# Dilated attention with queries and keys ordered by parity in two of its three groups

## Chip, core and metric

The kernel runs on one core of a Trainium2 chip. The metric is the device time of one execution in microseconds (us); a kernel's time is the median of its runs. The core has a matrix engine (PE, TensorE; its weight loads are listed apart as PEld), a vector engine (DVE), a scalar engine (ACT), GpSimd (POOL) and a queue engine (SP) that issues most transfers. Each engine executes its own instructions in order and waits on semaphores for the others.

## What is computed

Two blocks of transformer layers on 256 tokens of width 1024. The change touches one stage, the attention of the second layer of the first block, with 16 heads of 64 dimensions and three groups of keys. In short:

```python
DIL_CONFIGS = ((128, 1), (512, 4), (2048, 16))       # (window, dilation)

def dilated_group(q, k, v, window, dilation):
    """query t attends t, t-d, t-2d, ..., t-window"""
    ...
    logits = jnp.where(valid[None, None], logits, -jnp.inf)
    lse = jax.nn.logsumexp(logits, axis=-1)
    p = jnp.exp(logits - lse[..., None])
    return jnp.einsum("bhqk,bqkhd->bqhd", p, vb), lse

def dilated_attention(h, cos, sin, w_in, q_gain, k_gain, w_out):
    proj = (h @ w_in).reshape(B, S, N_DIL_GROUPS, 3, H, hd)
    for g, (window, dilation) in enumerate(DIL_CONFIGS):
        q = apply_rope(rms_norm(proj[:, :, g, 0], q_gain[g]), cos, sin)
        k = apply_rope(rms_norm(proj[:, :, g, 1], k_gain[g]), cos, sin)
        o, lse = dilated_group(q, k, proj[:, :, g, 2], window, dilation)
        ...
    alpha = jax.nn.softmax(jnp.stack(lses, axis=0), axis=0)
    o = jnp.sum(alpha[..., None] * jnp.stack(outs, axis=0), axis=0)
    return o.reshape(B, S, H * hd) @ w_out
```

Weighting the groups by their denominators is the same as one softmax over the scores of all three groups side by side, and that is what the kernel does. With dilations 4 and 16 a query meets only keys whose position differs from its own by an even number.

## The kernel before

A planner (`Plan`, `Program`) writes one list of steps. Five functions (`sp_program`, `pe_program`, `act_program`, `dve_program`, `pool_program`) then walk over that list, and each emits its engine's part. So the order on every engine is the order of the list; the waits are tokens (semaphore, value) that the planner gives out, among them `self.free[bank]`, the token after which one of the eight PSUM banks may be written again. A bank holds 512 fp32 values per partition. Banks G0 to G3 and D0 to D3 are used.

Weights stream through six slots (`raw`); ACT and DVE split each into a high and a low half (`whi`, `wlo`, line 1674 for DVE), and three matmuls (high x high, low x high, high x low) stand for one fp32 product. This is nearly all of the program.

The dilated stage goes over 8 heads at a time (`hh` 0 and 1). For each half:

- `dil_in` runs nine times (group g, part r: queries, keys, values). `token` multiplies tokens by a weight unit: 48 matmuls with a 128x128 piece of `xhi` or `xlo` (tokens t*128 to t*128+127) as the stationary operand and 512 weight columns moving. Queries and keys then pass through `head_norm`, are transposed on PE (`head_turn`, line 1453) into D0 and D1, and ACT copies them to `dqT` or `dkT` (64 dimensions of two heads x 256 tokens, four such pairs). Values are copied by ACT to `dv` (`keep_v`).
- `dil_attn` runs `attention` over eight steps p: pair of heads c = p // 2, query tile qt = p % 2. Tile qt has 128 queries and kl = 128 * (qt + 1) keys per group, so n = 384 or 768 scores per query. In `step_of(p)` the list gets: `scores(p)` and the two `bias` steps (DVE adds the mask `dmask` and takes the row's minimum, line 1774), `values(p - 2)`, then for each head w `turn` of the step before (PE transposes the weights `S`, line 1418, and ACT copies them to `PT`) and `exp` of this step (ACT), and the two `weigh` steps (DVE: reciprocal, line 1779, and product, line 1782). `values` multiplies `dv` by `PT` into G2 or G3; after the second query tile of a pair ACT copies the output (`doT`, or `xhi` in half 1, with `xlo` by DVE at line 1786).

For n = 768 a head's scores take two banks: `score_bank` returns D0 for the first head of every step and D2 for the second, and `turn` uses G0 and G1 together. All matmuls stand in the profile under line 1265, all ACT operations under line 1487, since helpers emit them; the tiles' names tell them apart. Matmuls on plain fp32 are recorded twice, transposes once.

Of the kernel before, what the change touches and what calls it, by code (L numbers as in the profile page):

```python
# [6 lines left out]
F32 = mybir.dt.float32  # L7
# [34 lines left out]
class Plan:  # L42
# [150 lines left out]
    def token(self, need):  # L193
        b0, b1 = self.next_pair()
        bank_free = [self.free[b0], self.free[b1]]
        for k0 in (0, 4):
            pc = self.take()
            tok = self.ev("pe", "piece")
            self.add("token", b0=b0, b1=b1, k0=k0, c=pc["c"], w_lo=pc["w_lo"], need=[need(k0 + kk) for kk in range(4)],
# [184 lines left out]
    def attention(self, name, klen, ready, emit, bias_ready=None, row=False, ng=1, compact=False, after=None):  # L384
# [3 lines left out]
        def score_bank(p, w):  # L388
            if compact:
                return D0 + w  # L390
            return D0 + 2 * w if ng > 1 else D0 + 2 * (p % 2) + w

        def scores(p):
            kl = klen(p % 2)
            n = kl * ng
            nb = -(-n // 512)
            banks = [score_bank(p, w) for w in range(2)]
            bank_free = [self.free[banks[w] + b] for w in range(2) for b in range(nb)]
            tok = self.ev("pe", "score")
            self.add("scores", name=name, p=p, kl=kl, n=n, nb=nb, banks=banks, bank_free=bank_free, row=row,  # L400
                     ready=ready[:-1] if first[0] else [])
            first[0] = False
            for w in range(2):
                j = 2 * p + w
                td = self.ev("dve", "biased")
                self.add("bias", name=name, j=j, n=n, nb=nb, bank=banks[w], score=tok, s_free=self.s_free[j % 4],
                         ready=bias_ready(2 * (p // 2) + w) if bias_ready else None)
                for k in range(nb):
                    self.free[banks[w] + k] = td
# [12 lines left out]
        def turn(j):  # L422
            n = rec[j][1]
            bt = G0 if n > 512 else G0 + j % 2
            banks = (G0, G1) if n > 512 else (bt,)
            tok, te = self.ev("pe", "turned"), self.ev("act", "pt")
            self.add("turn", name=name, j=j, n=n, bt=bt, nb=len(banks), weighed=rec[j][0], bank_free=[self.free[b] for b in banks],
                     turned=tok, pt_free=self.pt_free[j % 2])
            self.s_free[j % 4] = tok
            for b in banks:  # L430
                self.free[b] = te
# [47 lines left out]
    def emit_split(self, dst, c0, res):  # L479
        def emit(c, bank, tok):  # L480
            hi, lo = self.ev("act", "o_hi"), self.ev("dve", "o_lo")
            self.add("o_split", dst=dst, c=c0 + c, bank=bank, value=tok, o_hi=hi)
# [11 lines left out]
    def mix_attention(self, hh, name, compact, **kw):  # L494
# [8 lines left out]
        self.attention(name, lambda qt: P * (qt + 1), self.at, self.emit_split("x", 4, res), **kw)  # L503
# [85 lines left out]
class Program(Plan):  # L589
# [62 lines left out]
    def dil_attn(self, hh):  # L652
        self.mix_attention(hh, ("dil", hh), compact=False, ng=3)
# [79 lines left out]
    def na_attn(self, i):  # L733
        self.ya_split = [None] * 4
        steps = self.attention(("na", 0), lambda qt: T, self.nat, self.emit_split("ya", 0, self.ya_split),
# [371 lines left out]
def build(nc, a, out):  # L1107
    root = ExitStack()
    with root:
# [72 lines left out]
        with ExitStack() as c:  # L1182
# [8 lines left out]
            dil_mask = named("dmask", [P, 1152], F32, c)  # L1191
            dil_gn = named("dgn", [P, 2, 3, 64], F32, c)
            attn["dil"] = scratch(c, 768)
# [47 lines left out]

        def angle(n):
            return rp[:, n, :, :]
# [858 lines left out]
```

## Time and profile before

| | us |
|---|---|
| median of 3 runs | 2361.69 |
| lowest, highest | 2361.56, 2369.41 |
| the profiled execution's own time | 2364.49 |
| its span (first to last instruction) | 2363.2 |
| attention of half 0, in the span | about 965.7 to 1010.7 |
| attention of half 1, in the span | about 1120.1 to 1165.5 |

The page of the profile gives each engine's busy time and share of the span, the chain of work that ended last, and the costliest groups of instructions. PE is busy for 2260.6 us (96%), DVE for 1327.0, ACT for 1155.3. The ends of matmuls are modelled, so a busy PE is not PE at its peak; the starts are measured, and the distance from one start to the next is the better measure of pace. PEclk is the share of the full TensorE clock that was granted.

### The profile page before, as it was taken

To read this page: it belongs to the slowest core of one execution; us is meant where nothing else is said; L and a number is where in the kernel's file an instruction comes from. 1 tells how busy PE (TensorE), PEld (TensorE's weight loads), DVE (VectorE), ACT (ScalarE), POOL (GpSimd) and SP (SyncE) were. 2 spreads that over 40 slices of the span, in tenths; PEclk is the share of its full clock that TensorE was granted. 3 is DMA by queue.
4 is the path that set the end of the run, shared out by engine and by line. 5 is a ranking of instruction groups with operands and counts; after the bars stand their busy time and mean duration, and the time that the engine had idled before them with its cause. 6 is when DMAs were issued, how large, how long until landed. Compare 5 with 4: busy or idle time off the path is not lost.

```text
span 2363.2 us, 38278 instructions
## 1 busy us (share of the span) xinstructions
PE 2260.6 (96%) x16752; PEld 2060.3 (87%) x16752; DVE 1327.0 (56%) x1763; ACT 1155.3 (49%) x1348; POOL 57.2 (2%) x72
## 2 busy tenths in 40 slices
PE   6999998999999999899899999999999999999998
PEld 3999866999999987677699997899999988989998
DVE  2543565544455466657555445556786555667873
ACT  3443565543444354544554335654555456436553
POOL 2000000000000000000000011000000020000000
PEclk9999999999999999999999999999999999999999
DMA  8767562666575756345165555433655363445550
GB/s 311 236 229 289 196 250 68 218 223 231 187 252 196 266 192 247 128 150 205 56 214 183 192 196 175 161 125 125 211 182 191 126 233 132 154 143 179 179 196 19
DMA packets 273590, 439.75 MB, mean 186 GB/s; under 512 B 10656, under 2 KB 147152, under 8 KB 273296
## 3 DMA queue, kind: packets, MB, share of 16 engines
q1 hardware_dynamic: 270880, 429.07, 52.6%
q0 software_dynamic: 2256, 7.12, 0.9%
q8 instruction: 132, 2.16, 0.4%
q10 hardware_dynamic: 288, 1.11, 0.1%
q14 instruction: 34, 0.28, 0.0%
HBM read 436.22 MB, written 1.05 MB: 185 GB/s over the span
## 4 chain that ended last, share of the span: by engine, by line
PE 89%; ACT 5%; DVE 3%; DMA 1%; issue 1%; SPq 0%; POOL 0%; ACTq 0%; POOLq 0%; DVEq 0%
PE ps L1265 86%; ACT whi L1487 1%; DVE wlo L1674 1%; PE ps L1418 1%; ACT PT L1487 1%; PE ps L1365 1%; PE ps L1453 1%; DMA raw<-in_mod_w 1%; ACT xhi L1487 1%; PE ps L1428 1%; ACT L1487 1%; ACT S L1487 0%; DMA raw<-in_fox_w_in 0%; SPq L1254 0%; ACT x L1487 0%
## 5 line engine op out<-in xcount | busy, mean ns | idle before, releaser
L1674 DVE TENSOR_TENSOR wlo<-raw,whi 128x2048 fp32r<-128x2048 f32 x339 | 769.0, 2275 | 584.8 <-ACT whi L1487 584.6
L1487 ACT ACTIVATE whi<-raw 128x2048 fp32r<-128x2048 f32 x339 | 640.7, 1895 | 422.4 <-PE ps L1265 387.1
L1265 PE MATMUL ps<-xhi,whi 128*128 128x256 f32 x2888 | 733.5, 286 | 14.8 <-ACT xhi L1487 11.4
L1265 PE MATMUL ps<-xhi,wlo 128*128 128x256 f32 x2888 | 727.9, 284 | 0.0
L1265 PEld LDWEIGHTS ps<-xhi,whi 128*128 128x128 f32 x2888 | 555.7, 192 | 29.1 <-issue 27.6
L1265 PEld LDWEIGHTS ps<-xhi,wlo 128*128 128x128 f32 x2888 | 555.8, 192 | 0.3
L1265 PE MATMUL ps<-xlo,whi 128*128 128x256 f32 x2888 | 471.0, 284 | 3.6 <-DVE xlo L1892 3.4
L1265 PEld LDWEIGHTS ps<-xlo,whi 128*128 128x128 f32 x2888 | 401.4, 192 | 4.3 <-DVE xlo L1892 3.8
L1265 PE MATMUL ps<-hhi,whi 128*128 128x256 f32 x1056 | 299.0, 283 | 0.9 <-DVE modc L1687 0.9
L1265 PE MATMUL ps<-hlo,whi 128*128 128x256 f32 x1056 | 298.5, 283 | 0.0
L1265 PE MATMUL ps<-hhi,wlo 128*128 128x256 f32 x1056 | 297.5, 282 | 0.0
L1265 PE MATMUL ps<-whi,xhi 128*128 128x512 f32 x608 | 242.1, 398 | 7.0 <-DVE wlo L1674 4.5
L1265 PE MATMUL ps<-wlo,xhi 128*128 128x512 f32 x608 | 237.7, 391 | 0.0
L1265 PEld LDWEIGHTS ps<-hhi,whi 128*128 128x128 f32 x1056 | 199.6, 189 | 5.0 <-issue 3.4
L1265 PEld LDWEIGHTS ps<-hhi,wlo 128*128 128x128 f32 x1056 | 199.1, 189 | 0.1
L1265 PEld LDWEIGHTS ps<-hlo,whi 128*128 128x128 f32 x1056 | 197.9, 187 | 0.0
L1265 PE MATMUL ps<-whi,xlo 128*128 128x512 f32 x608 | 187.9, 390 | 0.0
L1265 PEld LDWEIGHTS ps<-whi,xhi 128*128 128x128 f32 x608 | 114.8, 189 | 37.1 <-issue 8.5
L1265 PEld LDWEIGHTS ps<-whi,xlo 128*128 128x128 f32 x608 | 114.3, 188 | 24.5
L1265 PEld LDWEIGHTS ps<-wlo,xhi 128*128 128x128 f32 x608 | 114.8, 189 | 22.4
L1487 ACT ACTIVATE e<-ps 128x512 f32<-128x512 f32 (+1 forms) x48 | 30.4, 634 | 158.3 <-PE ps L1265 158.2
L1487 ACT ACTIVATE hhi<-e 128x512 fp32r<-128x512 f32 x66 | 41.7, 632 | 110.0 <-DVE e L1936 71.2
(222 smaller groups left out, 1999.6 us busy)
## 6 DMA issues: line engine op xcount, KB each, us to landing
raw<-in_mod_w SPq DMA_DIRECT2D x72, 1024.0 KB, 9.2
raw<-in_w_in SPq DMA_DIRECT2D x52, 1024.0 KB, 4.9
raw<-in_ffn_w_gate SPq DMA_DIRECT2D x88, 512.0 KB, 6.5
raw<-in_ffn_w_up SPq DMA_DIRECT2D x88, 512.0 KB, 7.8
raw<-in_ffn_w_down SPq DMA_DIRECT2D x44, 1024.0 KB, 6.7
raw<-in_w_up SPq DMA_DIRECT2D x88, 512.0 KB, 4.7
raw<-in_dil_w_in SPq DMA_DIRECT2D x36, 1024.0 KB, 5.9
raw<-in_w_down SPq DMA_DIRECT2D x22, 1024.0 KB, 4.8
```

Of the source, the lines that this page charges most:

```text
L1265: return nc.tensor.matmul(o, lhs, rhs, start=start, stop=stop, skip_group_check=True)
L1365: ins = nc.tensor.transpose(ps[:, s["bank"], m * P:(m + 1) * P], mrow[:, m * P:(m + 1) * P], ident[:, :])
L1418: ins = nc.tensor.transpose(o, w["S"][:, s["j"] % 4, b * P:(b + 1) * P], ident[:, :])
L1428: ins = nc.tensor.transpose(ps[:, D2, h * T + b * P:h * T + (b + 1) * P], w["S"][:, j, b * P:(b + 1) * P], ident[:, :])
L1453: ins = nc.tensor.transpose(ps[:, D0 + c // 2, (c % 2) * T + t * P:(c % 2) * T + (t + 1) * P], tms[s["name"]][:, t, c * P:(c + 1) * P], id ...
L1487: return nc.scalar.activation(o, i, func, **kw)
L1674: V.tensor_tensor(wlo[:, s["c"], 0:s["n"]], raw[:, s["slot"], 0:s["n"]], whi[:, s["c"], 0:s["n"]].bitcast(F32), ALU.subtract).then_inc(sem ...
```

## The change

In groups 1 and 2 (dilations 4 and 16) queries and keys are put in order by parity, even positions first. The scores of these groups are computed for pairs of equal parity alone. For query tile qt this takes, per head and group, two matmuls (parity r = 0, 1) of 64 queries by kl / 2 keys in place of one of 128 by kl. The scores of a head are now n = 2 * kl = 256 or 512, so they fit into one bank.

- `score_bank` returns D0 + 2 * (p % 2) + w, so steps of even and odd p use different banks; `turn` uses one bank, G0 + j % 2, for every tile.
- The scores after the first kl are laid out in blocks of 128: 64 keys of group 1, then 64 keys of group 2. Transposed, a block has group 1's weights on partitions 0 to 63 and group 2's on 64 to 127. To match, `keep_v` of groups 1 and 2 fills `dv` of 1 and 2 crosswise, in two copies of 64 partitions each; a values matmul sums over both groups at once, for 64 queries of one parity.
- `token` for the values of groups 1 and 2 takes its tokens by parity: the stationary operand is every second column of `xhi` or `xlo`.
- `head_turn` writes all queries (group 0 too) in the order of parity within each tile of 128, and the keys of groups 1 and 2 in the order of parity over all 256; ACT reads the transposed values in PSUM with a step of two.
- The outputs come out in the order of parity within each tile of 128. ACT and DVE put them back when they write `doT`, `xhi` and `xlo` (`scattered`, `gathered`).
- The mask has 768 columns in place of 1152, in the new order.

```diff
@@ planner
-    def token(self, need):
+    def token(self, need, by_parity=False):
...
         def score_bank(p, w):
             if compact:
                 return D0 + w
-            return D0 + 2 * w if ng > 1 else D0 + 2 * (p % 2) + w
+            return D0 + 2 * (p % 2) + w
 
         def scores(p):
             kl = klen(p % 2)
-            n = kl * ng
-            nb = -(-n // 512)
+            n = 2 * kl if dilated else kl
             banks = [score_bank(p, w) for w in range(2)]
-            bank_free = [self.free[banks[w] + b] for w in range(2) for b in range(nb)]
+            bank_free = [self.free[b] for b in banks]
...
         def turn(j):
             n = rec[j][1]
-            bt = G0 if n > 512 else G0 + j % 2
-            banks = (G0, G1) if n > 512 else (bt,)
+            bt = G0 + j % 2
...
-        b0, b1, tok = self.token(self.need_x)
+        b0, b1, tok = self.token(self.need_x, by_parity=r == 2 and g > 0)
@@ PE, token
+            def tokens(t, kc, half, by_parity):
+                return (t[:, kc, :].rearrange("p (i r) -> p r i", r=2)[:, half, :] if by_parity else
+                        t[:, kc, half * P:(half + 1) * P])
@@ PE, scores
                     for g, (qT, kT, _) in enumerate(groups(s["name"])):
-                        for w in range(2):
-                            bk, off = s["banks"][w] + (g * kl) // 512, (g * kl) % 512
-                            ins = mm(ps[:, bk, off:off + kl], qT[64 * w:64 * w + 64, c, qt * P:(qt + 1) * P],
-                                     kT[64 * w:64 * w + 64, c, 0:kl], True, not s["row"])
+                        if g == 0:
+                            for w in range(2):
+                                h = slice(64 * w, 64 * w + 64)
+                                ins = mm(ps[:, s["banks"][w], 0:kl], qT[h, c, qt * P:(qt + 1) * P], kT[h, c, 0:kl], True,
+                                         not s["row"])
+                            continue
+                        for r in range(2):
+                            for w in range(2):
+                                h = slice(64 * w, 64 * w + 64)
+                                o = ps[64 * r:64 * r + 64, s["banks"][w], kl:2 * kl].rearrange("p (f g i) -> p g f i", g=2, i=64)
+                                ins = mm(o[:, g - 1, :, :], qT[h, c, qt * P + 64 * r:qt * P + 64 * r + 64],
+                                         kT[h, c, P * r:P * r + kl // 2].rearrange("p (f i) -> p f i", i=64), True, True)
@@ PE, values
+                    for f in range(nb if dilated else 0):
+                        b = nb + f
+                        for r in range(2):
+                            for w in range(2):
+                                hd, o = 2 * c + w, 64 * r
+                                ins = mm(ps[64 * w:64 * w + 64, s["bank"], qt * P + o:qt * P + o + 64],
+                                         every[1 + f][2][:, r, hd * 64:(hd + 1) * 64], PT[:, w, b * P + o:b * P + o + 64],
+                                         False, f == nb - 1)
@@ ACT, head_turn
+                    if s["dst"][0] == "dil" and s["dst"][1] == "q":
+                        act(dst[:, :, :].rearrange("p c (t r i) -> p (c t) r i", t=2, r=2),
+                            turned.rearrange("p b (c t i r) -> p (b c t) r i", c=2, t=2, r=2), ACT.Copy).then_inc(sem["head_kept"])
@@ ACT, keep_v
+                    if s["name"] in (("dil", 1), ("dil", 2)):
+                        h = 64 * s["name"][1] - 64
+                        act(qkv["dil", "v", 1][h:h + 64, :, :], ps[0:64, s["b0"]:s["b0"] + 2, :], ACT.Copy)
+                        act(qkv["dil", "v", 2][h:h + 64, :, :], ps[64:P, s["b0"]:s["b0"] + 2, :],
+                            ACT.Copy).then_inc(sem["v_kept"])
```

PE's instructions in steps 3 and 4 of half 0, before (S are the scores and then the weights of one head, PT their transpose, ps is PSUM; 128x256 is the output's shape, x5 a count, and "waits" names the semaphores: biased by DVE, pt by ACT, weighed by DVE):

```order
L1265 MATMUL ps<-dkT,dqT 128x256 [waits biased]
L1265 MATMUL ps<-dkT,dqT 128x256 x5
L1265 MATMUL ps<-PT,dv 64x128 [waits pt]
L1265 MATMUL ps<-PT,dv 64x128 x11
...
L1418 MATMUL ps<-ident,S 128x128 [waits weighed]
L1418 MATMUL ps<-ident,S 128x128 x5
L1418 MATMUL ps<-ident,S 128x128 [waits pt,weighed]
L1418 MATMUL ps<-ident,S 128x128 x5
```

The same place now:

```order
L1268 MATMUL ps<-dkT,dqT 128x256 [waits biased]
L1268 MATMUL ps<-dkT,dqT 128x256
L1268 MATMUL ps<-dkT,dqT 64x2x64 x8
L1268 MATMUL ps<-PT,dv 64x128 [waits pt]
L1268 MATMUL ps<-PT,dv 64x128 x3
L1268 MATMUL ps<-PT,dv 64x64 x8
...
L1432 MATMUL ps<-ident,S 128x128 [waits weighed]
L1432 MATMUL ps<-ident,S 128x128 x3
L1432 MATMUL ps<-ident,S 128x128 [waits weighed]
L1432 MATMUL ps<-ident,S 128x128 x3
```

Scores go from 6 to 10 matmuls, values stay at 12, the transposes of a head go from 6 to 4, and the second head's transposes no longer wait for ACT's copy (pt). Over the whole program PE has the same order otherwise.

PE at the head of half 0's attention, before (mod_row is ACT's copy out of bank D2 or D3, head_kept its copy of the transposed keys):

```order
L1265 MATMUL ps<-dkT,dqT 128x128 [waits mod_row,head_kept]
L1265 MATMUL ps<-dkT,dqT 128x128 x5
L1265 MATMUL ps<-dkT,dqT 128x256 [waits mod_col,biased]
L1265 MATMUL ps<-dkT,dqT 128x256 x5
L1418 MATMUL ps<-ident,S 128x128 [waits hn_mul,weighed]
```

and now:

```order
L1268 MATMUL ps<-dkT,dqT 128x128 [waits head_kept]
L1268 MATMUL ps<-dkT,dqT 128x128
L1268 MATMUL ps<-dkT,dqT 64x64 x8
L1268 MATMUL ps<-dkT,dqT 128x256 [waits mod_col,mod_row]
L1268 MATMUL ps<-dkT,dqT 128x256
L1268 MATMUL ps<-dkT,dqT 64x2x64 x8
L1432 MATMUL ps<-ident,S 128x128 [waits hn_mul,weighed]
```

The scores of step 1 have moved ahead of the bias of step 0: they no longer wait for it.

ACT ahead of the same attention, before:

```order
L1487 ACTIVATE dkT<-ps 128x1024
L1487 ACTIVATE dv<-ps 128x1024
L1487 ACTIVATE whi<-raw 128x2048
L1487 ACTIVATE mrow<-ps 128x512
L1487 ACT_TABLE_LOAD
```

and now:

```order
L1509 ACTIVATE dkT<-ps 128x1024
L1509 ACTIVATE dv<-ps 64x1024 x2
L1509 ACTIVATE whi<-raw 128x2048
L1509 ACTIVATE mrow<-ps 128x512
L1509 ACT_TABLE_LOAD
```

The copy of the values has become two, ahead of the weight split (`whi`) and of everything that attention asks of ACT.

## Rows read from the trace of the kernel before

**Rows 1.** Stretches: length; PE, PEld, DVE, ACT, POOL busy us; PEclk, DMA share, GB/s.
```profile
850.00:965.00 115.00, 113.76 (x561) 89.90 (x563) 80.73 (x111) 59.03 (x59) 1.65 (x3) 1.00 0.62 226
...
965.67:976.80 11.13, 5.55 (x43) 4.20 (x42) 7.00 (x15) 7.35 (x13) 0.00 (x0) 0.85 1.00 365
...
985.72:994.64 8.92, 7.23 (x79) 5.73 (x79) 5.45 (x17) 5.89 (x14) 0.00 (x0) 1.00 0.01 2
...
1003.56:1010.73 7.17, 5.28 (x49) 4.33 (x49) 1.11 (x3) 2.39 (x4) 0.00 (x0) 0.81 0.01 2
...
1120.14:1131.52 11.38, 6.92 (x43) 5.28 (x42) 6.71 (x20) 8.45 (x17) 0.00 (x0) 0.67 0.53 176
```

**Rows 2.** Chain of waits, part of a cycle of half 0: start us, us, what.
```profile
983.28 0.49 PE ps L1418 x3
...
983.79 0.49 ACT PT L1487
984.28 0.91 ACT S L1487 x2
985.20 0.39 ACT PT L1487
```

**Rows 3.** Timeline of PE, half 0: start us, us, line, op, count [idle before].
```profile
963.75 1.92 PE L1265 MATMUL ps<-raw,csil 128*32 128x512 f32 x16
...
980.25 1.57 PE L1265 MATMUL ps<-dkT,dqT 64*128 64x256 f32 x12
...
981.75 1.53 PE L1265 MATMUL ps<-PT,dv 128*64 128x128 f32 x24
...
983.21 0.88 PE L1418 MATMUL ps<-ident,S 128*128 128x128 f32 x6
...
985.72 0.88 PE L1265 MATMUL ps<-PT,dv 128*64 128x128 f32 x12 [0.47 <-ACT PT L1487]
...
986.53 0.87 PE L1418 MATMUL ps<-ident,S 128*128 128x128 f32 x6
...
988.39 0.85 PE L1418 MATMUL ps<-ident,S 128*128 128x128 f32 x6 [0.99 <-ACT PT L1487]
```

**Rows 4.** ACT, whole span, by shape: busy us, mean ns of one, idle before.
```profile
L1487 ACT ACTIVATE S<-S,nm 128x256 f32<-128x256 f32 x48 | 23.9, 501 | 5.2 <-DVE nm L1774 5.1
...
L1487 ACT ACTIVATE S<-S,nm 128x768 f32<-128x768 f32 x16 | 14.9, 929 | 0.0
...
L1487 ACT ACTIVATE PT<-ps 128x512 f32<-128x512 f32 x20 | 12.0, 599 | 33.0 <-PE ps L1428 33.0
...
L1487 ACT ACTIVATE PT<-ps 128x256 f32<-128x256 f32 x12 | 4.5, 379 | 6.6 <-PE ps L1428 4.4 <-PE ps L1418 2.2
```

**Rows 5.** DVE, whole span, by shape.
```profile
L1782 DVE TENSOR_SCALAR S<-S,ri 128x256 f32<-128x256 f32 x48 | 18.8, 391 | 1.7
...
L1774 DVE CUSTOM_DVE_ANT_0 S<-ps,dmask 128x768 f32<-128x768 f32 x16 | 14.6, 952 | 2.9 <-PE ps L1265 2.9
L1774 DVE CUSTOM_DVE_ANT_0 S<-ps,nbias 128x256 f32<-128x256 f32 x32 | 12.3, 421 | 4.7 <-PE ps L1265 4.7
...
L1782 DVE TENSOR_SCALAR S<-S,ri 128x768 f32<-128x768 f32 x16 | 9.9, 621 | 0.6
```

**Rows 6.** Timeline at the head of half 0's attention.
```profile
964.78 1.02 ACT L1487 ACTIVATE dv<-ps 128x1024 f32<-128x1024 f32 x1
...
968.23 0.94 PE L1265 MATMUL ps<-dkT,dqT 64*128 64x128 f32 x12 [2.55 <-ACT mrow L1487]
969.84 0.55 DVE L1774 CUSTOM_DVE_ANT_0 S<-ps,dmask 128x384 f32<-128x384 f32 x1
```

**Rows 7.** Timeline of a projection: starts of a load and of two matmuls.
```profile
1012.54 0.19 PEld L1265 LDWEIGHTS ps<-wlo,xhi 128*128 128x128 f32 x1
1012.76 0.40 PE L1265 MATMUL ps<-wlo,xhi 128*128 128x512 f32 x1
...
1013.00 0.39 PE L1265 MATMUL ps<-whi,xhi 128*128 128x512 f32 x1
```

More of the change, by code:

```diff
@@ L198, in token @@
             tok = self.ev("pe", "piece")
-            self.add("token", b0=b0, b1=b1, k0=k0, c=pc["c"], w_lo=pc["w_lo"], need=[need(k0 + kk) for kk in range(4)],
+            self.add("token", by_parity=by_parity, b0=b0, b1=b1, k0=k0, c=pc["c"], w_lo=pc["w_lo"], need=[need(k0 + kk) for kk in range(4)],
                      bank_free=bank_free if k0 == 0 else [])
@@ L382, in attn_begin, with attention @@
         self.pt_free = [None] * 2
-    def attention(self, name, klen, ready, emit, bias_ready=None, row=False, ng=1, compact=False, after=None):
+    def attention(self, name, klen, ready, emit, bias_ready=None, row=False, dilated=False, compact=False, after=None):
         rec = []
@@ L405, in scores @@
                 td = self.ev("dve", "biased")
-                self.add("bias", name=name, j=j, n=n, nb=nb, bank=banks[w], score=tok, s_free=self.s_free[j % 4],
+                self.add("bias", name=name, j=j, n=n, bank=banks[w], score=tok, s_free=self.s_free[j % 4],
                          ready=bias_ready(2 * (p // 2) + w) if bias_ready else None)
-                for k in range(nb):
-                    self.free[banks[w] + k] = td
+                self.free[banks[w]] = td
                 rec.append([td, n, kl])
@@ L477, in attention, with emit_split @@
         return []
-    def emit_split(self, dst, c0, res):
+    def emit_split(self, name, dst, c0, res):
         def emit(c, bank, tok):
             hi, lo = self.ev("act", "o_hi"), self.ev("dve", "o_lo")
-            self.add("o_split", dst=dst, c=c0 + c, bank=bank, value=tok, o_hi=hi)
+            self.add("o_split", name=name, dst=dst, c=c0 + c, bank=bank, value=tok, o_hi=hi)
             self.free[bank] = lo
@@ L734, in na_attn @@
         self.ya_split = [None] * 4
-        steps = self.attention(("na", 0), lambda qt: T, self.nat, self.emit_split("ya", 0, self.ya_split),
+        steps = self.attention(("na", 0), lambda qt: T, self.nat, self.emit_split("na", "ya", 0, self.ya_split),
                                bias_ready=lambda h: self.bias_ready[h // 2], compact=True)
@@ L1240, in flat, with scattered, gathered @@
             return t[:, k0:k1, :].rearrange("p k n -> p (k n)")
+        def scattered(o, name):
+            return o.rearrange("p (t i r) -> p t r i", t=2, r=2) if name == "dil" else o
+        def gathered(o, name):
+            return o.rearrange("p (t r i) -> p t r i", t=2, r=2) if name == "dil" else o
         def angle(n):
@@ L1438, in pe_program @@
                     PT = attn[s["name"][0]]["PT"]
-                    tot = nb * len(every)
-                    for b in range(tot):
+                    dilated = len(every) > 1
+                    for b in range(nb):
                         for w in range(2):
@@ L1443, in pe_program @@
                             ins = mm(ps[64 * w:64 * w + 64, s["bank"], qt * P:(qt + 1) * P],
-                                     every[b // nb][2][:, b % nb, hd * 64:(hd + 1) * 64], PT[:, w, b * P:(b + 1) * P],
-                                     b == 0, b == tot - 1)
+                                     every[0][2][:, b, hd * 64:(hd + 1) * 64], PT[:, w, b * P:(b + 1) * P],
+                                     b == 0, b == nb - 1 and not dilated)
+                    for f in range(nb if dilated else 0):
[6 more added lines that the diff above has]
+                                         False, f == nb - 1)
                     ins.then_inc(sem["value"])
@@ L2025, in constants @@
     parts = []
+    parity, nth = q // 64, q % 64
     for qt in range(2):
-        for window, dil in ((128, 1), (512, 4), (2048, 16)):
-            d = (q[:, None] + P * qt) - np.arange(P * (qt + 1))[None, :]
+        kl = P * (qt + 1)
+        query = (P * qt + 2 * nth + parity)[:, None]
+        same = 2 * np.arange(64)[None, :] + parity[:, None]
+        keys = [(np.broadcast_to(np.arange(kl), (P, kl)), 128, 1)]
+        for half in range(qt + 1):
+            keys += [(same + P * half, 512, 4), (same + P * half, 2048, 16)]
+        for key, window, dil in keys:
+            d = query - key
             parts.append(np.where((d >= 0) & (d <= window) & (d % dil == 0), 0.0, BIG).astype(np.float32))
```

55 lines of the change are left out of this document (31 added, 24 removed).

## The prediction, made before the changed kernel ran

> **What bounds the kernel now.** I read the page first, then the busy time by stretch. Nearly everywhere PE sets the time: in the projections ahead of the first dilated attention it is busy for 113.76 of 115 us, while ACT works for 59.03 and DVE for 80.73 [rows 1]. The two dilated attentions are the exception. Half 0's runs from 965.67 to 1010.73, 45.1 us; half 1's has the same instructions. In a steady stretch of two steps (a cycle: one pair of heads, both query tiles) PE works for 7.23 of 8.92 us, ACT for 5.89, DVE for 5.45 [rows 1]: no engine is full, so a loop of waits sets the pace.
>
> The chain of waits shows the loop: transposes on PE, the copy of the weights to PT on ACT (0.49 us), an exponential (0.91), the second copy (0.39), values on PE [rows 2]. After the tile of 768 scores it is worse: the second head's transposes wait 0.99 us for the first head's copy, since both use banks G0 and G1 (at 988.39) [rows 3]. Transfers are out of it: in the steady cycle the DMA engines are busy for 0.01 [rows 1], because the six slots are full. What attention gives back should therefore come off the end.
>
> **Pace of PE.** 12 value matmuls take from 981.75 to 983.21, 1.46 us, and 6 take from 985.72 to 986.53, 0.81 [rows 3]. So one costs (1.46 - 0.81) / 6 = 0.108 us, and a block costs another 0.16 for the change to the next kind of matmul. One of 128 columns on half the array in 0.108 us, two halves side by side, means 0.216 if it were alone. Six score matmuls of 256 columns take 1.50 us (980.25 to 981.75): 0.216 each and 0.20 for the change. The modulation matmuls, which use a quarter of the array's columns, are 8 of 512 columns in 1.92 us (at 963.75) [rows 3]; alone they would be 8 x 4 x 0.216 = 6.9, so four do run side by side.
>
> **The change part by part, per cycle.**
>
> Transposes: 18 become 12, at 0.108 each: 0.65 us less on PE. Some of it is in the loop (below).
>
> Values: of 18 matmuls of 128 columns 6 stay, 12 now have 64 columns. At half the price each this saves 0.22 us for the first tile and 0.43 for the second, and makes the blocks 0.59 and 1.03 us. If a floor per instruction held, nothing is saved.
>
> Scores: 2 matmuls stay per step, 4 become 8 of a quarter of the area, which use a quarter of the array (64 rows, 64 columns). No row shows that shape. Bounds for the second tile: with four side by side 2 x 0.216 + 8 x 0.054 + 0.20 = 1.06; with two, 1.49; one at a time, 2.36. One more change of shape adds 0.16 to each. For the first tile half the work: 0.79 to 1.44, where before it was 0.85. I take four side by side, as in the modulation row: 1.22 and 0.79. The scores have a window to hide in, while ACT works.
>
> The Trainium skill speaks against this part: "TensorEngine Tiling (Array Packing)", Key Properties, says that changing the tiling mode drains the engine, and a step now has one such change more. Its 64×64 mode has four tiles that run at once. The trace agrees as far as it goes: the block's fixed 0.16 and 0.20 us above are such changes, and they are small against the wait removed.
>
> Elementwise work shrinks by a third. From the slopes between 256 and 768 columns [rows 4, 5]: an exponential of 512 takes 0.715 us, bias 0.69, product 0.47; a copy of 512 is 0.60; those of 256 are 0.50, 0.42, 0.39 and 0.38. ACT's cycle falls to about 5.1 us, DVE's to about 4.4.
>
> Banks: scores of the next step no longer wait for the bias of this one, nor the second head's transposes for the first's copy. What is late next? The PE-ACT loop: values of the first tile 0.59; transposes 0.87 (at 986.53) [rows 3] less two of 0.108, and 0.04 to the copy's start, 0.69; copy 0.51 until the next can start; exponential 0.50; copy 0.60; hand-over 0.13 (ACT's copy of 985.20 ends at 985.59, PE starts at 985.72 [rows 2, 3]); values 1.03; transposes beside the copy of the output 0.45; copy 0.28; exponential 0.70; copy 0.38; hand-over 0.13. Sum 5.99. The DVE-ACT loop (product, next bias, exponential, copy, exponential, for both tiles) is 0.47 + 0.39 + 0.69 + 0.42 + 2 x (0.50 + 0.715) + 0.60 + 0.38 = 5.4, with reciprocals and hand-overs, which I estimate at 0.9, 6.3. PE alone: scores 2.0, values 1.6, transposes 1.6, so 5.2. I take 6.3 for the cycle; 5.9 is the least, and with one-at-a-time scores about 7.5 the most.
>
> Three whole cycles per half: 2 x 3 x (8.92 - 6.3) = 15.7 us.
>
> Head of the attention: scores of step 0 no longer wait 2.55 us for ACT's mrow copy out of a bank they don't use now [rows 6], and those of step 1 not for the bias. But keep_v is two copies of as many columns; I take each as long as the one (1.02 [rows 6]; the least would be half of it). They stand ahead of the weight split, whose DVE part stands ahead of the bias. So the bias starts at 970.9, not 969.84 [rows 6]. Then bias to 971.3, two exponentials and products until 973.1, bias of step 1 ready at 973.9, exponential, copy and hand-over: values of step 0 at 975.1, against 976.80 [rows 1]: 1.7 us gained. In half 1 (11.38 us now) the same, and more of it at half clock: 2.0. The two other double copies are covered by PE's full projections.
>
> Tail: after the last cycle 7.17 us in half 0 [rows 1]. Now 0.59 + 0.69 + 0.51 + 0.60 + 0.13 + 1.03 = 3.55, and about 1 more where PE is at half clock (0.81 there [rows 1]): 2.6 less. For half 1 I take about the same, 5.0 in all.
>
> Reordering copies: ten copies of transposed queries and keys read PSUM with a step of two. Nothing in the trace shows such a read; bounds are the present 1.02 us and twice that. Eight lie under projections with ACT half idle; the last of each half is in the path: 0 to 2.0 in all, I take the middle, 1.0. Outputs written with a step of two: 0.38 us each, same bounds, hidden beside transposes.
>
> Strided stationary operand: 4 units x 48 = 192 matmuls of 512 columns. They start 0.23 us apart (1012.76, 1013.00) and a load takes 0.19, under the matmul before [rows 7]. Lower bound nothing; at twice the duration (0.38) 0.15 x 192 = 29 us; I take nothing, the value of the only rows with such loads. The mask's smaller transfer is nothing: DMA has room.
>
> In the Trainium skill, "Advanced Engine Details and Errata", SBUF Cachelines, lines are 16 bytes and two hits per line suffice; a step of two fp32 gives just two, so by it these loads cost nothing. By its section PSUM Cachelines a line there is 8 bytes, so a step of two fp32 uses one element of each, and the last reordering copies would stand in the sum with 2.0 instead of 1.0. No row of this case shows either.
>
> **Sum.** 15.7 + 3.7 + 5.0 - 1.0 = 23.4 us. The profiled execution took 2364.5 (span 2363.2 and 1.3 around it), so 2341; it was 2.8 above the median of 2361.7, and against that median the forecast is 2338.5.
>
> **Rivals.**
>
> A. Quarter-array matmuls gain nothing from each other, or PE's instructions (88 per cycle in place of 78) come no faster. For it: the shape is new here. Against: modulation. Cycle 7.5 us: 2 x 3 x 1.4 = 8.5, with head and tail 16 us, 2346.
>
> B. Slower: strided weight loads. If a step of two makes a load three times as long, 0.57 us, PE starts every 0.57 instead of 0.23 in 192 matmuls: 65 us lost, 2404. It eats the gain from 0.23 + 23.4 / 192 = 0.35 us per load; a result slower than before by 0.5% needs 0.41. For it: no row with a step. Against: so large a factor.
>
> C. PE falls to half clock inside the cycles, because it has less to do. For it: at the head, with PE busy 6.92 of 11.38 us, the clock was 0.67 [rows 1]. Against: 7.23 of 8.92 kept 1.00, and 5.2 of 6.3 is the same share. At half clock PE alone needs some 9.5 us: 2 x 3 x 0.6 = 3.5 lost, head and tail gained (8.7 - 1.0): 2357.
>
> D. The gain is hidden anyway, for the next stage waits for something else. Against: 0.01 DMA share, full slots. about 2360.
>
> **Chances.** Forecast 0.79, its own range 2332 to 2345; A 0.10; B 0.05; C 0.04; D 0.02. 0.5% is 11.8 us, about what a measurement tells from no change. Faster by more 0.88, within 0.06 (C, D and the edge of B), slower 0.06. Range for 8 in 10: 2331 to 2350, which takes in A.
>
> **What would show it.** Cycles from one block of first-tile values to the next near 6.3 us, at clock 1.00; no wait of transposes for PT; scores of step 1 before the bias of step 0; score blocks of the second tile near 1.2 us; the 64-row copies at 1.0; matmuls of by-parity tokens still 0.23 apart. Wrong, if these last are further apart, if copies of dqT exceed 2 us, or if cycles stay above 8 us.

## Result and profile after

The changed kernel takes 2339.2 us (median of 4 runs, 2337.9 to 2341.9), the kernel before 2361.9 beside it. The ratio is 0.9894, 95% interval 0.9882 to 0.9906: 25 us (22 to 28) less. The two medians themselves are 22.7 us apart. The forecast was 2338.5 us. The profiled execution took 2341.9 us, with a span of 2340.6, 22.6 less than before.

The table compares starts in the two traces (us).

| stretch | before | after | gained | predicted |
|---|---|---|---|---|
| ahead of the dilated stage (its first matmul at 854.62, 855.97) | | | -1.35 | 0 |
| four by-parity units, first to last start of a unit | 10.75 | 11.05 | -1.2 | 0 |
| head, half 0 (copy of dkT to first values) | 12.94 | 11.45 | 1.5 | 1.7 - 0.5 |
| head, half 1 | 11.34 | 9.47 | 1.9 | 2.0 - 0.5 |
| three cycles, half 0 | 26.76 | 19.25 | 7.5 | 7.9 |
| three cycles, half 1 | 28.05 | 19.57 | 8.5 | 7.9 |
| tails (last first-tile values to next projection) | 7.17, 5.88 | 3.82, 3.82 | 5.4 | 5.0 |
| first unit of half 1's projections, to the start of the next | 11.71 | 11.37 | 0.3 | - |
| sum | | | 22.6 | 23.4 |

The first row is not the change, since both kernels run the same instructions up to there. It is what is left of two differences: within the first 50 us of the span the changed kernel's execution gains 4.0 us (why is open), and between 300 and 412 us, around the attention ahead of this stage, it loses 5.4, with 0.92 of the clock granted where the kernel before had 0.98. Stretches of the kernel before, then of the changed one (length; PE, PEld, DVE, ACT, POOL busy; PEclk, DMA share, GB/s):

```profile
300.00:412.00 112.00, 103.39 (x624) 77.57 (x621) 63.97 (x165) 64.27 (x132) 0.00 (x0) 0.98 0.44 156
```

```profile
300.00:412.00 112.00, 105.74 (x601) 79.24 (x601) 60.45 (x162) 61.26 (x128) 0.00 (x0) 0.92 0.40 140
```

The changed kernel's heads, steady cycle, tail and half 1's first cycle:

```profile
965.88:977.33 11.45, 6.72 (x81) 3.43 (x81) 5.89 (x16) 9.69 (x15) 0.00 (x0) 0.79 0.83 304
984.22:990.40 6.18, 5.60 (x88) 4.17 (x89) 4.24 (x17) 4.48 (x14) 0.00 (x0) 1.00 0.01 3
996.58:1000.40 3.82, 2.96 (x45) 2.39 (x45) 0.95 (x3) 1.75 (x4) 0.00 (x0) 1.00 0.00 0
1110.15:1119.62 9.47, 4.58 (x64) 2.96 (x64) 5.02 (x19) 8.51 (x17) 0.00 (x0) 0.80 0.62 204
1119.62:1126.83 7.21, 6.71 (x92) 5.29 (x89) 4.42 (x18) 4.30 (x14) 0.00 (x0) 0.79 0.01 2
```

The steady cycle (984.22 to 990.40) takes 6.18 us, where [rows 1] have 8.92. PE's share rose from 7.23 of 8.92 to 5.60 of 6.18. The two heads ran at 0.79 and 0.80 of the clock, and in half 1 so did the first cycle (7.21); half 0's first cycle took 6.89 us at 0.86.

PE in the steady cycle of the changed kernel, start and duration, idle time before and its releaser in brackets:

```profile
984.22 0.67 PE L1268 MATMUL ps<-PT,dv 128*64 128x128 f32 x12 [0.51 <-ACT PT L1509]
984.82 1.39 PE L1432 MATMUL ps<-ident,S 128*128 128x128 f32 x8
986.14 1.30 PE L1268 MATMUL ps<-dkT,dqT 64*128 64x256 f32 x20
987.37 1.12 PE L1268 MATMUL ps<-PT,dv 128*64 128x128 f32 x24
988.42 0.66 PE L1432 MATMUL ps<-ident,S 128*128 128x128 f32 x4
989.01 0.88 PE L1268 MATMUL ps<-dkT,dqT 64*128 64x128 f32 x20
```

Start to start: values 0.60 and 1.05 us (0.59 and 1.03 predicted), scores of the second tile 1.23 (1.22). The second head's transposes no longer wait 0.99 us for PT [rows 3]; what is left is 0.51 us for PT ahead of the first tile's values. The chain of waits through the same cycle (start, duration, what; "S x2" is an exponential with the reading of its sum):

```profile
984.81 0.18 DVE ri L1818
...
985.01 0.50 DVE S L1821
...
985.55 0.66 PE ps L1432 x4
986.21 2.31 PE ps L1268 x44
...
988.54 0.42 ACT doT L1509
988.95 0.33 ACT PT L1509
989.28 0.70 ACT S L1509 x2
989.98 0.27 ACT PT L1509
990.26 0.71 ACT S L1509 x2
```

It is one loop through all three engines: the second head's exponential, its reciprocal and product on DVE, its transposes, the scores and values of the second tile on PE, then on ACT the copy of the output (doT), a copy to PT, the first head's exponential and the other copy to PT. The predicted loops, PE-ACT (5.99) and DVE-ACT (6.3), each hold a part of it, and neither holds the second tile's scores.

### The profile page after: what moved, and what is told of

It is laid out like the page before. It is cut to its first block, busy times and chain, and to the rows that moved or that the text cites. A ratio compares the mean times of both kernels' runs of the same rounds, so it can differ in the third digit from the quotient of the medians.

```text
span 2340.6 us, 38441 instructions
## 1 busy us (share of the span) xinstructions
PE 2247.2 (96%) x16832; PEld 2049.3 (88%) x16832; DVE 1317.4 (56%) x1763; ACT 1148.6 (49%) x1352; POOL 61.2 (3%) x72
## 3 DMA queue, kind: packets, MB, share of 16 engines
q0 software_dynamic: 2192, 6.92, 0.8%
HBM read 436.02 MB, written 1.05 MB: 187 GB/s over the span
## 4 chain that ended last, share of the span: by engine, by line
PE 89%; ACT 5%; DVE 3%; DMA 1%; issue 1%; SPq 0%; POOL 0%; ACTq 0%; POOLq 0%; DVEq 0%
PE ps L1268 86%; ACT whi L1509 1%; DVE wlo L1713 1%; ACT xhi L1509 1%; PE ps L1475 1%; PE ps L1372 1%; DMA raw<-in_mod_w 1%; ACT S L1509 1%; ACT L1509 1%; PE ps L1442 1%; PE ps L1432 1%; DMA raw<-in_fox_w_in 0%; ACT PT L1509 0%; SPq L1257 0%; ACT x L1509 0%
```

## Experiments

Each ratio is to the kernel before, run beside the experiment. Totals of one kernel differ by some us between executions, with the clock granted in stages that no kernel here touches. So each experiment is read first from one stretch of its trace, from the dilated stage's first matmul to the last values of half 1. That is 309.37 us before and 285.99 in the changed kernel: 23.4 less.

**One pair of banks for the transposes (e1), for the scores (e2), for both (e9).**

```diff
@@ e1, transposes of 512 columns also wait for the other head's copy
                     q.wait_ge(s["bank_free"])
+                    q.wait_ge(s["other"])
@@ e2
-            return D0 + 2 * (p % 2) + w
+            return D0 + 2 * w if dilated else D0 + 2 * (p % 2) + w
```

> Takes away the second buffer of the transposes alone: a head's transposes of 512 columns also wait for the copy of the other head's weights, as they did before. Smaller tiles and the second pair of score banks stay. Theory S (the smaller tiles give most of the gain): after the first head's transposes (0.66 us with the product) the second's start some 0.5 to 0.6 us later, and this wait is paid once per cycle, since it stands in the loop: cycles 6.7 us in place of 6.18, in all 8 x 0.55 = 4.4 us given back of some 23, so ratio to the kernel before 0.991. Theory B (the free banks give most of it): the cycle goes back towards 8 us and more than 10 us are given back, ratio 0.994 or more. Theory H (the wait is hidden by exponentials): cycle 6.2, ratio 0.989.

> Takes away the second pair of score banks alone: scores of every step go to D0 and D2, so those of step p+1 wait for the bias of step p. Tiles and transposes stay as changed. Theory S: scores of the second tile start at most 0.1 us later (bias of the first tile is done when PE comes to them), those of the first tile about 0.4 us later, beside exponentials that they don't delay: cycle 6.2 to 6.4 us; at the head of each attention about 0.5 to 1.5 us more. In all 1 to 4 us given back, ratio 0.990 to 0.991. Theory B: cycle 7 us or more, ratio 0.993 or more.

> Both banks' doublings are taken away together (e1 and e2 in one kernel); only the smaller tiles and the matmuls of equal parity stay. If the two add up, the stretch from the first projection of the dilated stage to the last values of half 1 is 286.0 + 9.8 + 4.7 = 300.5 us (309.4 before): the smaller tiles alone give 8.9 of the 23.4 us and the banks 14.5; ratio about 0.996. If they overlap (the second head's transposes and the next scores wait in the same time), 297 us and ratio 0.994: smaller tiles 12, banks 11.

The stretch in e1, e2 and e9:

```profile
853.42:1149.25 295.83, 274.08 (x1744) 215.98 (x1744) 189.13 (x332) 156.44 (x212) 0.00 (x0) 0.96 0.50 179
```

```profile
852.51:1143.17 290.66, 272.21 (x1744) 215.05 (x1745) 189.07 (x332) 155.57 (x212) 0.00 (x0) 0.96 0.51 182
```

```profile
855.25:1150.45 295.20, 271.71 (x1745) 214.01 (x1745) 189.19 (x332) 156.24 (x212) 0.00 (x0) 0.96 0.51 179
```

e1 gives back 9.8 us (ratio 0.9929, 0.9913 to 0.9946). Theory S was right on the steady cycle, 6.85 us (PE below), and wrong on the sum. It allowed 0.55 us for each of 8 cycles; the first cycle of each half took 10.2 and 9.9 us, at 0.59 and 0.61 of the clock.

```profile
984.96 0.67 PE L1269 MATMUL ps<-PT,dv 128*64 128x128 f32 x12 [0.51 <-ACT PT L1511]
985.56 0.66 PE L1434 MATMUL ps<-ident,S 128*128 128x128 f32 x4
987.00 0.63 PE L1434 MATMUL ps<-ident,S 128*128 128x128 f32 x4 [0.78 <-ACT PT L1511]
987.56 1.30 PE L1269 MATMUL ps<-dkT,dqT 64*128 64x256 f32 x20
...
991.81 0.67 PE L1269 MATMUL ps<-PT,dv 128*64 128x128 f32 x12 [0.51 <-ACT PT L1511]
```

The third line shows the wait that came back. e2 gives back 4.7 us (ratio 0.9921, 0.9906 to 0.9937), mostly at the heads (13.36 and 11.00 in place of 11.45 and 9.47); its steady cycles are 6.29 to 6.37. Both together (e9) give back 9.2, not the sum of 14.5, and less than the 11 of the second guess; the ratio is 0.9941 (0.9927 to 0.9955).

Most of the 5.3 us between 14.5 and 9.2 is granted clock and not an overlap of waits. The first cycle of half 1, in e1 and then in e9:

```profile
1122.30:1132.20 9.90, 8.61 (x93) 6.35 (x89) 4.59 (x18) 4.42 (x14) 0.00 (x0) 0.61 0.01 2
```

```profile
1126.39:1133.24 6.85, 5.63 (x94) 4.18 (x89) 4.39 (x18) 4.40 (x14) 0.00 (x0) 1.00 0.00 0
```

With the second pair of score banks gone as well, the cycle is 3 us shorter, at full clock. The two first cycles together are longer than the changed kernel's by 6.0 us in e1, 0.6 in e2 and 2.3 in e9: 4.3 of the 5.3. Why e1's ran so long at half clock, no run shows. The waits themselves overlap by little: e1 adds 0.67 us to a steady cycle, e2 0.11 to 0.19, both together again 0.67 (988.07 to 994.92 in e9), so there the scores' wait falls into time that the transposes' wait has already made, but over four steady cycles that is 0.7 us.

So of 23.4 us in the stretch the free banks give 9.2 and the smaller tiles 14.2, as these traces stand. No run parts the 14.2 further, into PE's smaller matmuls and the shorter work of DVE and ACT. As e1 and e9 stand 0.6 apart, with other stretches of half clock, I would not read these closer than 1 or 2 us.

**Shape and number of score matmuls (e3, e4).**

```diff
@@ e3, one matmul of 128 queries in place of two of 64
-                        for r in range(2):
-                            for w in range(2):
...
+                        for w in range(2):
+                            h = slice(64 * w, 64 * w + 64)
+                            o = ps[:, s["banks"][w], kl:2 * kl].rearrange("p (f g i) -> p g f i", g=2, i=64)
+                            ins = mm(o[:, g - 1, :, :], qT[h, c, qt * P:(qt + 1) * P],
+                                     kT[h, c, 0:kl // 2].rearrange("p (f i) -> p f i", i=64), True, True)
@@ e4
-                                h = slice(64 * w, 64 * w + 64)
+                                h = slice(0, 64)
```

> Scores of groups 1 and 2 as 4 matmuls per step on 64 rows x 128 columns in place of 8 on 64 x 64; all 128 queries of a tile meet the keys of even position alone, so the queries of odd position have the wrong keys. The streamed work is the same if four quarter tiles do run side by side (8 x N / 4 = 4 x N / 2), and there is no change of shape within the block. Theory M (a change of shape costs 0.16 us): score block of the second tile 1.06 us in place of 1.23, of the first 0.65 to 0.70 in place of 0.79; cycle 6.0, since the second tile's block is in the loop; total 1 to 1.5 us less than the changed kernel. Theory N (the change of shape costs nothing, quarter tiles are a bit slower than four side by side): same direction but a block that starts its last matmuls at a uniform distance. Theory I (the number of instructions sets the block): 0.9 us or less.

> The quarter-array scores of both heads read their operands from partitions 0 to 63, so that only two of the four quarters of the array are used (both heads get the first head's scores in groups 1 and 2). Same instructions and sizes. Theory Q (four quarters run side by side when they may): now two do, each 128-column quarter matmul of the second tile takes 0.108 of PE's time in place of 0.054, block 1.23 + 8 x 0.054 = 1.66 us; first tile 0.79 + 0.22 = 1.0; cycle 6.18 + 0.43 = 6.6; total 3 to 4 us more than the changed kernel, ratio about 0.991. Rival P (what pairs up are columns alone, rows do not matter): blocks and cycle unchanged.

PE in a steady cycle of e3, then of e4:

```profile
982.47 1.15 PE L1268 MATMUL ps<-dkT,dqT 64*128 64x256 f32 x12
983.56 1.12 PE L1268 MATMUL ps<-PT,dv 128*64 128x128 f32 x24
```

```profile
987.40 1.77 PE L1268 MATMUL ps<-dkT,dqT 64*128 64x256 f32 x20
989.10 1.12 PE L1268 MATMUL ps<-PT,dv 128*64 128x128 f32 x24
```

e4's block is 1.70 us in place of 1.23 and its cycle 6.65 in place of 6.18 (stretch 290.79; ratio 0.9912, 0.9896 to 0.9928). The 0.47 more is what 8 matmuls cost when they run two abreast and not four: theory Q holds, and it is paid in full, since this block stands in the loop. e3's block is 1.09 and its cycle 6.04, 0.14 less. That is the price of one more change of shape (theory M), since the time is lost where the shape changes. From the last matmul of group 0 to the first of groups 1 and 2 it is 0.31 us in the changed kernel and 0.21 in e3, to the next one 0.16 and 0.11. Behind that the starts are 0.11 us apart in both, and in the changed kernel four matmuls start together each time, within 0.02 us. By the number of instructions (12 records for 20) the block would have fallen further. The Trainium skill, "TensorEngine Tiling (Array Packing)", Key Properties, has both: tiles operate independently, and a change of mode drains the engine. The trace agrees with both, by the 1.23 us beside 1.70 and by the 0.14. e3's total (ratio 0.9896, 0.9879 to 0.9913) can't show 0.8 us in six cycles, and its stretch (285.84) doesn't either.

**Stationary operands with a step (e8, e5).**

```diff
@@ e8
-        b0, b1, tok = self.token(self.need_x, by_parity=r == 2 and g > 0)
+        b0, b1, tok = self.token(self.need_x, by_parity=False)
@@ e5: step 4 and 8 in half 0, 16 and 3 in half 1
+                    k0 = min(kc, NC - (by_parity + 1) // 2)
+                    a = t[:, k0:, :].rearrange("p k n -> p (k n)")[:, 0:P * by_parity]
+                    return a.rearrange("p (i r) -> p r i", r=by_parity)[:, half, :]
```

> Values of groups 1 and 2 from tokens in their given order (stationary operand without a step; the values of the wrong tokens). Theory F: units 10.75 in place of 11.05 us, 4 x 0.30 = 1.2 us less than the changed kernel, 2338.0. Rival: the 0.3 us per unit is not the step but the longer double copy behind it: units stay at 11.05.

> The stationary operand of the four values units of groups 1 and 2 is read with other steps in place of 2: half 0 group 1 step 4, group 2 step 8; half 1 group 1 step 16, group 2 step 3 (wrong tokens, same number of matmuls and loads). In the changed kernel a unit of 48 matmuls with step 2 takes 11.05 us from first to last start, without a step 10.75. Theory L (a load pays per 16-byte line of 4 fp32 that it touches once it uses fewer than two elements of each): steps 4, 8 and 16 are alike and slower, up to 0.38 per load in place of 0.19: as the load then outlasts the matmul it becomes the pace, 0.38 us each, unit 18 us; step 3 in between. Theory F (a step costs the same small amount whatever its length, about 6 ns per matmul): all four units 11.05. Theory G (cost grows with the distance): 4 < 8 < 16.

In e8 the four units take 10.75 us: the 0.30 us per unit are the step, 1.2 in all. The stretch fell only by 0.7, because half 1's first cycle was slower (7.7 for 7.2, at 0.74 of the clock). The ratio, 0.9912 (0.9898 to 0.9925), is no better than the changed kernel's; a gain this small can't be read from it. Weight loads with steps of 4, 8, 16 and 3 (e5, one unit each; count, busy us, mean ns):

```profile
L1268 PEld LDWEIGHTS ps<-whi,xlo 128*128 128x128 f32 x16 | 4.4, 316 | 0.0
...
L1268 PEld LDWEIGHTS ps<-whi,xlo 128*128 128x128 f32 x16 | 4.6, 330 | 0.0
...
L1268 PEld LDWEIGHTS ps<-whi,xlo 128*128 128x128 f32 x16 | 4.3, 300 | 0.0
...
L1268 PEld LDWEIGHTS ps<-whi,xlo 128*128 128x128 f32 x16 | 3.9, 253 | 0.0
```

and with step 1 and 2 in the changed kernel (units at 904.46 and 916.24):

```profile
L1268 PEld LDWEIGHTS ps<-whi,xlo 128*128 128x128 f32 x16 | 3.0, 188 | 0.6
...
L1268 PEld LDWEIGHTS ps<-whi,xlo 128*128 128x128 f32 x16 | 3.1, 194 | 0.6
```

The load's own time follows theory L in kind: nearly nothing up to two elements per 16 bytes, then 253, 316, 330, 300. But the unit takes 11.05, 11.21, 11.32, 11.73 and 11.25 us for steps 2, 3, 4, 8 and 16. Loads recorded as 316 ns go with matmuls that start 241 ns apart on average (11.32 / 47). So the pace is not the load's duration, as theory L had it, and F and G fail too: the price is neither fixed nor does it grow with distance. Each of these steps was measured in one unit only; e5's ratio is 0.9898 (0.9875 to 0.9921, two runs). The Trainium skill, "Advanced Engine Details and Errata", SBUF Cachelines, says that it takes two hits on a line to absorb the latency; the loads' durations agree (188 and 194 ns against 253 to 330), and step 2 cost 6 ns per matmul, not nothing.

**The second copy of the values (e6).**

```diff
-                    if s["name"] in (("dil", 1), ("dil", 2)):
+                    if False:
```

> Values of groups 1 and 2 are kept by one copy of 128 partitions in place of two of 64 (halves of the parities are not crossed, so the values stand in the wrong place). Each copy of 64 partitions takes 1.02 us, as long as the one. Theory: the second copy is in the path at the head of both attentions, ahead of the weight split and bias of half 0 and ahead of the output split and the table load of half 1: 1.0 us each, 2.0 in all, total 2337.2 against 2339.2. Rival: something else is late there (the transfer, the transposed keys), gain 0 to 0.5.

The heads take 10.16 and 8.03 us in place of 11.45 and 9.47: 1.3 and 1.4 less, and the stretch 2.8 less (283.18). The theory holds (it expected 2.0), and the price is a little above one copy: after a copy of 128 partitions the next starts 0.92 us later (968.53 behind 967.61 below), while the two copies of 64 take 2.07 from 966.93 to 969.00 and start 1.05 behind that of dkT (965.88). ACT at the head of half 0, of e6 and then of the changed kernel:

```profile
967.61 1.02 ACT L1509 ACTIVATE dkT<-ps 128x1024 f32<-128x1024 f32 x1 [4.50 <-PE ps L1475]
968.53 1.02 ACT L1509 ACTIVATE dv<-ps 128x1024 f32<-128x1024 f32 x1
969.44 1.91 ACT L1509 ACTIVATE whi<-raw 128x2048 fp32r<-128x2048 f32 x1
```

```profile
965.88 1.02 ACT L1509 ACTIVATE dkT<-ps 128x1024 f32<-128x1024 f32 x1 [4.50 <-PE ps L1475]
966.93 2.04 ACT L1509 ACTIVATE dv<-ps 64x1024 f32<-64x1024 f32 x2
969.00 1.91 ACT L1509 ACTIVATE whi<-raw 128x2048 fp32r<-128x2048 f32 x1
```

The ratio, 0.9896 (0.9880 to 0.9913), is no different from the changed kernel's.

**The order at the head (e7), mirrored banks (e10), and filled waits (e11, e12).**

```diff
@@ e7: begun adds the last values' copies; ensure() half 0's weight split, which take(2) keeps from being planned earlier
-            pc = self.take(ahead)
+            pc = self.take(2 if (i, u) == (1, 13) else ahead)
...
+            if begun and p == 0:
+                begun()
...
+            if hh == 0 and p == 8:
+                self.ensure()
+            if hh == 1 and p in (2, 4, 6, 8):
+                self.split_chunk(p // 2 - 1, ("dil", 1), self.o_ready[p // 2 - 1])
@@ e10, with e7
-            bt = G0 + j % 2
+            bt = (G2 if mirror else G0) + j % 2
-            bank = D3 if compact else G2 + c % 2
+            bank = D3 if compact else (G0 if mirror else G2) + c % 2
@@ e11, with e10: n = 4 and 6 in half 0; 4, 4 and 6 in half 1
+                    for _ in range(s["n"]):
+                        mm(ps[:, s["bank"], :], xhi[:, 7, 0:P], flat(xhi, 5, 7), True, True)
```

> The full computation. ACT's order at the head of the dilated attention: the last values' copies stand behind the exponentials of step 0; half 0's weight split behind step 8's copies; in half 1 the four splits of the kept output stand one each behind steps 2, 4, 6, 8 in place of ahead of step 0. Theory: the head is a queue on ACT and DVE that nothing in attention needs. Half 0: bias of step 0 some 4 us earlier, exponentials wait for the table load instead (about 2.7 us earlier), values of step 0 about 7.7 us behind the start of the keys' copy in place of 11.45: 3.7 us. Half 1: 2.6 us. Splits in the cycles fall into ACT's 1 us of idle time: 0 to 0.3 each lost. Total 2339.2 - 5.5 = 2333.7, ratio 0.987. Rival: the copies only move into the loop ahead of PT and the head gains less than 2 us; or the later transfer starves the next projection: 2339 or more.

> e7 and, in half 1, transposes in G2 and G3 and values in G0 and G1, since the last projected values of half 1 stand in G0 and G1 and there the first transposes waited 2.61 us for their copies. First transposes of half 1 at 3.8 us behind the start of the keys' copy in place of 5.80, the copies of PT right behind the values' copies: values of step 0 at 7.1 us in place of 7.75: 0.6 us less. Rival: half clock comes a little later and takes it back: 0.

> e10 and matmuls of 128x512 on xhi that nobody reads, put into PE's waits at the head of each attention: 4 behind the scores of step 1, 6 behind those of step 2, in half 1 also 4 ahead of the scores of step 0, 0.23 us each. Theory C (the granted clock falls to half because PE waits so much at the head, and this costs more than the wait): the granted clock stays 1.00 through both attentions; cycle from the first values to the next 6.2 to 6.9 us in place of 8.3 and 7.4 in e7, so 2 to 3 us less than e10; ratio 0.986 or less. Rival D (the clock falls all the same, and the fillers stand in the way at half pace): 1 to 3 us more than e10.

> The changed kernel as it is, with matmuls of 128x512 on xhi that nobody reads in PE's waits at the head: half 0 12 ahead of the scores of step 1 and 6 behind them, half 1 4 ahead of the scores of step 0 and 15 behind those of step 1, each set shorter than the wait it stands in. It prices the half clock in the changed kernel apart from the order on ACT. Theory C: granted clock 1.00 through both attentions; heads 0.6 us shorter each in place of 11.45 and 9.47 (transposes 0.60 for 1.18, scores beside them), first cycles 6.2 in place of 6.89 and 7.21: 2.9 us less in all, 2336.3, ratio 0.988. Rival: the heads hang on DVE and ACT alone and only the cycles gain, 1.7 us; or the clock falls later all the same, 0.

e7's heads are 8.48 and 7.75 us, 3.0 and 1.7 shorter (3.7 and 2.6 expected), and then its first cycles are longer. Two stretches of e7, the first cycle of each half:

```profile
970.38:978.70 8.32, 7.82 (x88) 5.92 (x89) 4.32 (x17) 4.46 (x14) 0.00 (x0) 0.67 0.65 236
...
1112.37:1119.80 7.43, 6.92 (x89) 5.49 (x89) 4.91 (x19) 4.78 (x15) 0.00 (x0) 0.77 0.01 2
```

Half 0's took 6.89 in the changed kernel. The time at half clock has moved from the head, where PE waits anyway, into the first cycle, where the loop runs through PE. So the stretch is 282.90, 3.1 less and not 5.5. The median, 2336.0 us, was expected at 2333.7. The ratio is 0.9876 (0.9859 to 0.9893), not clear of the changed kernel's. e10 makes half 1's head 7.18, 0.6 less than e7, as expected; stretch 282.12, ratio 0.9895 (0.9882 to 0.9909), where the total shows nothing of the 0.8.

e11 keeps the clock. The first cycle of each half, with the stretch of both:

```profile
974.56:980.62 6.06, 5.55 (x90) 4.16 (x89) 4.13 (x17) 4.36 (x14) 0.00 (x0) 1.00 0.85 313
...
1113.86:1120.00 6.14, 5.54 (x90) 4.15 (x89) 4.71 (x19) 4.75 (x15) 0.00 (x0) 1.00 0.00 0
...
856.05:1135.12 279.07, 271.62 (x1768) 214.12 (x1769) 188.58 (x331) 155.20 (x212) 0.00 (x0) 1.00 0.54 189
```

The stretch is 3.05 shorter than e10's, all of it in the two first cycles (6.06 and 6.14 for 8.04 and 7.45, while the heads are 0.1 longer), and 6.9 shorter than the changed kernel's. The median, 2335.0 us (2331.7 to 2336.1; ratio 0.9870, 0.9856 to 0.9884), is 5.3 below e10's 2340.4, measured beside it; the stretch accounts for 3.05 of that. e11 has the shortest stretch and the lowest ratio here. By the ratio alone it is not clear of e7 (0.9876), and its interval touches that of the changed kernel, whose own runs, at another time, were all above 2337.8. e12, the fillers in the changed kernel alone:

```profile
852.90:1136.79 283.89, 274.95 (x1782) 216.60 (x1782) 188.81 (x332) 155.81 (x212) 0.00 (x0) 1.00 0.53 186
```

It is 2.1 shorter than the changed kernel's, not the 2.9 of theory C: the heads 0.16 and 0.15, the first cycles 6.18 and 6.18 for 6.89 and 7.21. The first rival named in its expectation was right: heads hang on ACT and DVE, and there half clock costs next to nothing; in a cycle it costs. Its ratio is 0.9884 (0.9864 to 0.9904), not clear of the changed kernel's.

## Why the prediction held, step by step

- **Cycles.** 15.7 predicted, 16.0 measured. The estimate for a cycle, 6.3, was 6.18, and in part that is luck: the loop that sets the pace is neither of the two summed up. The prediction gave the scores "a window to hide in, while ACT works". The second tile's don't hide: their 1.23 us stand in the loop, and e4's 0.47 more in the block came out as 0.47 more in the cycle. The estimate of 0.9 for reciprocals and hand-overs lifted the DVE-ACT loop from 5.4 to 6.3, near the real one. Six cycles of 6.18 would have gained 16.4; 1.7 at half clock in the first cycles after, 1.3 before, make it 16.0. For size of tile and banks the prediction gave no split; it named the waits for PT and for the bias as what goes. By e9's trace these are 9.2 of 23.4 us, the smaller tiles 14.2.
- **Four quarters abreast (rival A).** 1.22 predicted, 1.23 measured, and e4 shows what two abreast cost. Rival A is refuted.
- **Heads.** 3.7 less 1.0 predicted, 3.4 measured. The mechanism was as told: scores of step 1 ahead of the bias, values' copies in the path. Two sizes were off. The second copies cost 1.3 and 1.4 us, not 1.02 (e6). The reordering copies cost nothing: those of dkT take 1023 ns on average (group 0's, without the step, as well as the others), of dqT 1026, where the kernel before has 1026 and 1028. The 1.0 us taken for them is refuted. So are the 2.0 that would have stood there by the Trainium skill, "Advanced Engine Details and Errata", PSUM Cachelines. That section speaks of matmuls; for ACT's reads of fp32 with a step of two the trace does not show such a price.
- **Tails.** 5.0 predicted, 5.4 measured. At half 0's end the clock was 1.00, where it had been 0.81 [rows 1]. The prediction counted on about 1 us of half clock there after the change, and the kernel before had lost 1.3 to it; at half 1's end, at full clock in both, the gain is 2.1. So 1.3 of the 5.4 come from the clock and not from shorter work.
- **Strided loads (rival B).** Taken at 0, measured 0.30 per unit, 1.2 in all. The rival's break-even of 0.41 us per load assumed that a longer load holds the matmuls apart by its own length. e5 shows that even a load of 0.33 us leaves a unit at 11.73 us; rival B's premise fell.
- **Half clock (rival C).** Not in steady cycles, as argued; but the head's half clock reaches into the first cycles (0.86 and 0.79), and it cost 1.7 us there (e12). Before, half 1's first cycle had paid as well (10.21 for 8.92).
- **Gain hidden (rival D).** Refuted: behind half 1 PE's starts in the two traces stay 22.2 to 22.9 us apart to the end.
- The forecast leaned on two errors that cancel: 1.2 us of strided loads were left out, and 1.0 of reordering copies was put in. (Its last sum is off by a little too: 2361.7 less 23.4 is 2338.3, not 2338.5.)

## What to carry to other kernels

When no engine is full, list the loop that the waits make through all engines; an instruction is worth its time only where it stands in that loop (the second tile's scores, not the first's). The gains of buffers freed at two places of one loop need not add up: try them together, and compare cycles at the same granted clock before calling the difference an overlap. After shortening a stretch look at the granted clock behind it, since a wait that costs nothing itself can send the next busy stretch to half clock; a few matmuls that nobody reads, set into the wait and shorter than it, took this away here.

## What the hardware showed

- fp32 score matmuls on 64 rows and 64 columns run four abreast: the block of 2 + 8 takes 1.23 us, two abreast 1.70, and one change of shape costs 0.14 (e3).
- A stationary operand with a step of 2 fp32 takes 194 ns to load for 188, with 3, 4, 8 and 16 it takes 253, 316, 330 and 300; the unit of 48 matmuls grows from 10.75 us to 11.05, 11.21, 11.32, 11.73 and 11.25 (e5, one unit each beyond step 2).
- ACT's copy of 64 partitions x 1024 takes 1015 ns, that of 128 x 1024 1018. Reads of PSUM with a step of two cost nothing (1023 and 1026 ns), writes of doT with one 407 ns for 388.
- Granted clock at the heads of the changed kernel: 0.79 and 0.80, with PE busy for 6.72 of 11.45 and 4.58 of 9.47 us. With unread matmuls in the waits (e12) it was 1.00, with 10.17 of 11.29 and 8.33 of 9.32 busy. The steady cycles kept 1.00 with 5.60 of 6.18.
- The fall can come behind the idle stretch: half 1's head in e7 kept 1.00 with PE busy for 3.56 of 7.75 us, and the cycle behind it, busy for 6.92 of 7.43, had 0.77. That cycle had 0.61 in e1 and 1.00 in e9, though e9 only adds a wait to e1.
